# A lag of six and eight pieces behind the first token half, the turn of h ahead of the last step, and a shorter expert selection

## The reference, cut to what matters

```python
merged = sigmoid(ga) * (ya @ w_branch_a) + sigmoid(gb) * (yb @ w_branch_b)
mix_out = merged @ w_out
ple = sigmoid(x @ w_ple_gate) * (p @ w_ple)
x = layer_norm(ALPHA * x + mix_out + ple, ln_g, ln_b)      # end of block 1
h = rms_norm(x, g_mix_norm) * (1 + scale_m) + shift_m      # block 2 begins
q_lat, kv_lat, k_rope, fq, fk, fv, f_logit, gate_a, gate_b = split(h @ w_in)
```

```python
choice = sigmoid(h @ w_router) + b_router
group_keep = top 4 of (sum of the two best choices in each group)
expert_idx = top_k(where(group_keep, choice, -1e30), 6)
```

## Time and profile before

| | |
|---|---|
| median of 3 runs | 1021.34 us (1021.08 to 1021.52) |
| the profiled execution | 1018.69 us, its span 1017.0 us |
| PE busy | 995.1 us (98%) |
| DVE, ACT, POOL busy | 586.9, 441.1, 380.0 us |
| mean granted TensorE clock | 0.998 of full |
| HBM read | 319.25 MB, 316 GB/s over the span |

### The profile page before, as it was taken

How to read it: one execution, slowest core, us unless ns; L and a number is a source line. 1 busy time by engine, 2 the same in 40 slices (tenths; PEclk the granted TensorE clock), 3 DMA queues, 4 the chain that set the end, 5 groups by cost and what they waited for, 6 DMA issues and landing times.

```text
span 1017.0 us, 14499 instructions
## 1 busy us (share of the span) xinstructions
PE 995.1 (98%) x5866; PEld 707.9 (70%) x5866; DVE 586.9 (58%) x1032; ACT 441.1 (43%) x731; POOL 380.0 (37%) x363
## 2 busy tenths in 40 slices
PE   9999999999999899999999999999999999999997
PEld 7878888888887787888787665655555564655553
DVE  4899768877966796866666333433333332333353
ACT  5645777656434664667344232222322232222213
POOL 2299999995993089698001100000000000000000
PEclk9999999999999999999999999999999999999999
DMA  9767666567675386565589899999999999999994
GB/s 330 310 223 252 231 208 231 209 215 285 232 239 203 140 301 211 203 202 170 196 329 407 351 426 428 423 427 427 426 427 426 426 424 428 425 429 423 427 425 180
DMA packets 36260, 322.31 MB, mean 317 GB/s; under 512 B 4160, under 2 KB 4192, under 8 KB 13664
## 3 DMA queue, kind: packets, MB, share of 16 engines
q1 hardware_dynamic: 28064, 291.94, 71.7%
q0 software_dynamic: 7840, 28.90, 8.7%
q10 hardware_dynamic: 288, 0.52, 0.1%
HBM read 319.25 MB, written 2.10 MB: 316 GB/s over the span
## 4 chain that ended last, share of the span: by engine, by line
PE 86%; DVE 7%; ACT 3%; DMA 2%; issue 1%; SPq 1%; ACTq 0%; DVEq 0%
PE ps L931 77%; PE ps L1312 6%; PE ps L935 4%; DVE rlo L1879 3%; DVE rt L1879 1%; DMA ring<-in_w_in 1%; ACT hl L1435 1%; DMA ring<-in_w_out 1%; DVE bs L1879 1%; ACT ex L1435 0%; DVE L L1879 0%; ACT L L1435 0%; SPq L803 0%; SPq L804 0%; ACT bs L1435 0%
## 5 line engine op out<-in xcount | busy, mean ns | idle before, releaser
L931 PE MATMUL ps<-hl,L 128*128 128x512 f32 (+1 forms) x1216 | 329.9, 393 | 5.1 <-DVE L L1879 4.1
L931 PEld LDWEIGHTS ps<-hl,L 128*128 128x128 f32 x1216 | 225.1, 188 | 54.5 <-issue 7.0
L1879 DVE TENSOR_TENSOR rlo<-ring,hl 128x1024 fp32r<-128x1024 f32 (+1 forms) x154 | 219.6, 1445 | 71.5 <-ACT hl L1435 70.8
L931 PE MATMUL ps<-slots_all,xe 128*64 128x256 f32 x2048 | 228.1, 381 | 0.0
L1435 ACT ACTIVATE hl<-ring 128x1024 fp32r<-128x1024 f32 (+1 forms) x154 | 160.3, 1055 | 115.3 <-PE ps L931 105.9
L931 PEld LDWEIGHTS ps<-slots_all,xe 128*64 128x64 f32 x2048 | 144.2, 137 | 74.6 <-issue 5.0
L931 PE MATMUL ps<-rlo,L 128*128 128x512 f32 (+1 forms) x608 | 187.5, 389 | 1.1 <-DVE rlo L1879 0.9
L859 POOL TENSOR_SCALAR mring<-mring,st 128x512 f32<-128x512 f32 x84 | 167.4, 1993 | 1.6
L931 PEld LDWEIGHTS ps<-rlo,L 128*128 128x128 f32 x608 | 113.8, 188 | 26.5 <-DVE rlo L1879 3.1
L921 POOL CAST two<-ident 64x64 fp32r<-64x64 f32 x104 | 20.5, 239 | 293.2 <-PE ps L931 275.6
L861 POOL TENSOR_TENSOR macc<-macc,mring 128x512 f32<-128x512 f32 x84 | 126.8, 1509 | 7.0
(11 more groups left out here) (248 smaller groups left out, 886.1 us busy)
## 6 DMA issues: line engine op xcount, KB each, us to landing
slots_all<-in_w_exp_gate SPq DMA_DIRECT2D x32, 2048.0 KB, 25.3
slots_all<-in_w_exp_up SPq DMA_DIRECT2D x32, 2048.0 KB, 26.7
slots_all<-in_w_exp_down SPq DMA_DIRECT2D x31, 2048.0 KB, 28.0
ring<-in_w_in SPq DMA_DIRECT2D x48, 1024.0 KB, 4.9
mring<-in_w_mod POOLq DMA_DIRECT2D x48, 512.0 KB, 4.0
ring<-in_w_out SPq DMA_DIRECT2D x8, 1024.0 KB, 7.1
ring<-in_w_ple_gate SPq DMA_DIRECT2D x4, 1024.0 KB, 5.6
ring<-in_w_branch_a SPq DMA_DIRECT2D x4, 1024.0 KB, 5.5
```

The source lines that it names most:

```text
L931: return e.matmul(o, l, r, start=start, stop=stop)
L1879: return e.tensor_tensor(o, a, b, op)
```

## The change

It does these things:

1. Two more `hl` buffers (`hl_more`) for all pieces up to `g0`, so eight instead of six; `ready_with` is worked out with them, so up to `g0` each conversion stands up to two pieces earlier in the streams of ACT and DVE.
2. `wo0 wo1` at a lag of 6 (14 steps); `c0` and `fq` become one run with a lag of 8 (16 steps).
3. PE: `merged_turn(1)` after step 4 of `wo`; `h_turn(0)` after step 12, ahead of the last half-piece; `mod_sum(9)` after the run; the six unread matmuls go; `h_turn(1)` after step 6 of the joined run.
4. ACT and DVE: their parts of the layer norm stand at other steps; the evacuations of `c0` and `fq` move inside the joined run, and the norm of the latents comes behind all its 16 steps.
5. `h3_turn(0)` after step 10 of `wp`, ahead of the last half-piece; `h3_shift` in two parts of two columns.
6. Selection: `pen` and one product fall away, ranks count from 1 instead of 0 so that a subtraction goes, selectors before the copy of the ranks, and `gather(0, 0..3)` ahead of `turn_ranks`.

```diff
+        hl_more = place("hl_more", [128, 2, 1024], F32R, at=pos[0])
-        BEHIND = (("bb0 bb1", 4), ("wo0 wo1", 4), ("c0", 4), ("om0 om1", 3), ("wp0 wp1", 4))
+        BEHIND = (("bb0 bb1", 4), ("wo0 wo1", 6), ("c0 fq", 8), ("om0 om1", 3), ("wp0 wp1", 4))
...
+        more_until = blocks["g0"][0]
+        hi_buf = [g % (NH + 2) if g < more_until else (g - npieces + 4) % NH for g in range(npieces)]
+        hi_before = [max((q for q in range(g) if hi_buf[q] == hi_buf[g]), default=None) for g in range(npieces)]
...
-            while at_piece < npieces and (at_piece < NH or used[at_piece - NH] < t) and all(
+            while at_piece < npieces and (hi_before[at_piece] is None or used[hi_before[at_piece]] < t) and all(
                     freed_by(q) <= t for q in range(pieces[at_piece][0] - NS + 1)):
...
-            project("wo0", L1, l_ready("mT"), {1: lambda: merged_turn(1)})
+            project("wo0", L1, l_ready("mT"), {4: lambda: merged_turn(1), 12: lambda: h_turn(0)})
             mod_sum(9)
-            h_turn(0)
-            w.wait_ge(*evacuated(two_before["c0"], 0))
-            for n in range(6):
-                mm(PS[bank_of["c0"]][:, 0:128], ident[:, :], ident[:, :], True, True)
-            project("c0", L0, h_ready, {2: lambda: h_turn(1)})
-            project("fq", L0, h_ready)
+            project("c0", L0, h_ready, {6: lambda: h_turn(1)})
             project("fk", L0, h_ready)
...
-            h3_turn(0)
+            project("wp0", L0, l_ready("mT2"), {1: lambda: merged_turn2(1), 10: lambda: h3_turn(0)})
...
+            gather(0, range(4))
             turn_ranks()
-            gather(0, range(4))
...
-            project("wo0", at={2: first_rows, 7: lambda: ln_square(0), 8: first_squares, 9: roots})
+            project("wo0", at={5: first_rows, 7: lambda: ln_square(0), 8: first_squares, 9: lambda: square_root(0)})
             h_round(0, 0)
+            ln_square(1)
             h_round(0, 4)
...
+            project("c0", at={3: second_rows, 6: second_h, 12: lambda: keep("c0", lambda m: PR[:, m, :], ACT.Copy)})
+            fox("fq", FQ)
...
+            project("wo0", at={3: lambda: wo(0, 0), 5: lambda: completed("mT", tokens=(1,)), 7: first_rows, 9: first_root,
+                               13: lambda: h_shift(0)})
+            wo(1, 1)
+            less_mean(1)
+            h_low(0, 0)
+            variance(1)
+            h_shift(4)
+            scale(1)
+            scaled(1, 0)
+            h_low(0, 4)
+            scaled(1, 1)
+            mod_sum(9)
...
+            project("c0", at={3: second_root, 5: lambda: pr_evac(0, PS[bank_of["c0"]][:, :]), 6: second_h,
+                              9: lambda: fox_evac("fq", FQ)(0, PS[bank_of["fq"]][:, :])})
...
-            mine(tt(kp, gsb[:, :, 0:8], gs[:, :, 0:8], ALU.not_equal))
-            mine(tsc(pen, kp, 1.0, 1e30, ALU.subtract, ALU.mult))
-                x = tt(w8[m], c8[m], spread(kp[:, m, :], 8), ALU.mult)
-                x = tt(w8[m], w8[m], spread(pen[:, m, :], 8), ALU.add)
+            mine(tt(left_out, gsb[:, :, 0:8], gs[:, :, 0:8], ALU.is_equal))
+                x = stt(w8[m], spread(left_out[:, m, :], 8), -1e30, c8[m], ALU.mult, ALU.add)
...
-            tsc(RK, RK, 1.0, None, ALU.subtract, None).then_inc(rk_set, 1)
```

More of the change, by code:

```diff
@@ L325, in two_blocks @@
         two_before = {name: order[n - 2] if n > 1 else None for n, name in enumerate(order)}
+        more_until = blocks["g0"][0]
+        hi_buf = [g % (NH + 2) if g < more_until else (g - npieces + 4) % NH for g in range(npieces)]
+        hi_before = [max((q for q in range(g) if hi_buf[q] == hi_buf[g]), default=None) for g in range(npieces)]
+        last_more = max(g for g in range(more_until) if hi_buf[g] >= NH)
         def hi_of(g):
-            return hl[:, (g - npieces + 4) % NH, 0:2 * pieces[g][2]].rearrange("p (k n) -> p k n", k=2)
+            b = hi_buf[g]
+            v = hl[:, b, :] if b < NH else hl_more[:, b - NH, :]
+            return v[:, 0:2 * pieces[g][2]].rearrange("p (k n) -> p k n", k=2)
         def ring_pair(i):
@@ L789, in load_early @@
                 if q == "shared":
+                    w.wait_ge(pe_w, both(last_more))
                     e.dma_start(w_shared, D["w_route_2"]).then_inc(shared_in, 16)
@@ L1541, in project @@
                         w.wait_ge(*((halves_in[i], 16) if g in (0, 2) else (slot_sem[i % NS], slot_at[i])))
-                        if g >= NH:
-                            w.wait_ge(pe_w, both(g - NH))
+                        if hi_before[g] is not None:
+                            w.wait_ge(pe_w, both(hi_before[g]))
                         act(hi_of(g), view, ACT.Copy).then_inc(hi, 1)
@@ L1659, in first_squares, with second_rows, second_h, fox @@
                 square(0, 1)
[L1661 to L1665 removed]
+            project("wo0", at={5: first_rows, 7: lambda: ln_square(0), 8: first_squares, 9: lambda: square_root(0)})
             h_round(0, 0)
[L1667 removed]
+            ln_square(1)
             h_round(0, 4)
[L1669 to L1673, removed]
+            def second_rows():
+                square(1, 0)
+                square(1, 1)
+                square_root(1)
+            def second_h():
+                h_round(1, 0)
+                h_round(1, 4)
+            project("c0", at={3: second_rows, 6: second_h, 12: lambda: keep("c0", lambda m: PR[:, m, :], ACT.Copy)})
+            def fox(name, buf):
+                if name != "fq":
+                    project(name)
+                done(name, 1)
+                act(heads(buf, 1, 66)[:, :, 0:64], PS[bank_of[name] + 1][:, :].rearrange("p (h d) -> p h d", d=64),
+                    ACT.Copy).then_inc(ev_a.sem, 1)
+            fox("fq", FQ)
             for base_ in (64, 136):
@@ L1676, in _ @@
                 act(st[:, base_ + 4:base_ + 6], st[:, base_ + 4:base_ + 6], ACT.Sqrt).then_inc(lat_a, 1)
-            def fox(name, buf):
-                project(name)
-                done(name, 1)
-                act(heads(buf, 1, 66)[:, :, 0:64], PS[bank_of[name] + 1][:, :].rearrange("p (h d) -> p h d", d=64),
-                    ACT.Copy).then_inc(ev_a.sem, 1)
             w.wait_ge(fz_v, 1)
@@ L2374, in first_rows, with first_root, second_root @@
                 scaled(0, 1)
-            def second_rows():
+            def first_root():
                 w.wait_ge(sq_a, 2)
                 mean_square(0, rt_v)
-                wo(1, 1)
+                wo(0, 1)
                 diagonal(0)
[L2381 to L2392, removed]
+            project("wo0", at={3: lambda: wo(0, 0), 5: lambda: completed("mT", tokens=(1,)), 7: first_rows, 9: first_root,
[10 more added lines that the diff above has]
+            mod_sum(9)
+            def second_root():
                 w.wait_ge(sq_a, 4)
@@ L2395, in third_rows, with second_h @@
                 diagonal(1)
[L2397 to L2400, removed]
+            def second_h():
+                h_low(1, 0)
+                h_low(1, 4)
             def pr_evac(m, b):
```

64 lines of the change are left out of this document (26 added, 38 removed).

## The result

The changed kernel takes 1036.74 us in the median of 4 runs (1034.21 to 1037.93); the kernel before took 1021.21 beside it (4 runs, 1019.57 to 1021.52). The ratio is 1.0148, 95% interval 1.0126 to 1.0171. The forecast was 1030.0 with a range of 1022.0 to 1035.5: the direction is right, the time lies above the range. The profiled execution took 1034.21 us, its span 1032.5 against 1017.0, and its mean granted clock is 0.988 against 0.998.

A forecast was written before the change was run, and what follows sets the result against it. PE was taken as the bound, busy 995.1 of 1017.0 us. Terms 4.3 + 0.6 - 0.7 + 4.3 + 1.0 - 0.75 = +8.75 on 1018.69 gave 1027.4, plus 2.65 to the median 1030.1, stated as 1030.0; range 1022 to 1035.5.

The forecast's parts named there:

- part 4: Latents: `lT` waits 4.1 us for the late norm, `fv` starts 4.3 later, `latents_up` another 1.0 later.
- F+15.4: Time counted from F, the start of `fk`: from about there DVE has four conversions, an evacuation and LT before `latents_up`.
- a rival with a chance of 0.12: Clock falls to half in PE's stops before `c0` and `lT`: up to +5 us on the sum, up to 1035; chance 0.12.
- two stops of 4 us: PE waits 4.0 us before `c0` and 4.1 before `lT`, both forecast in the sum.
- `c0` to `fk`: Joined run of `c0` and `fq`: 24.36 us before, 2.4 of waits become 1.7, so -0.7.
- My price per fall: Loss from one clock fall, 2.5 us, from 30 small matmuls at the start taking 6.25 us; two falls up to +5.
- start to `wo0`: Conversion of `wo1` waits for its load ahead of rounding `mT`: `wo0` starts at 318.3 instead of 313.98, +4.3.
- my own lower case of +1.5: The delay of `wo0` if loads land after 4.9 us instead of 7.7: +1.5 instead of +4.3.
- `wo0` to `c0`: 26.6 us of work, 1.7 of waiting before `h_turn(0)` and a 4.0 hole before `c0`: 32.3 against 31.65, +0.6.
- `h3_turn(0)`: In `wp`, one half-piece earlier: `wp(1,1)` comes 0.94 later, but the chain to `h3_turn(1)` has slack: 0, bound -0.9 to +0.9.
- selection's term: Fewer small operations before the ranks (0.33 us) and no 0.40 wait before `turn_ranks`: -0.75, lost again if expert loads come no earlier.
- the lags themselves: Without both +4.3 terms +0.9 is left, total +0.15: lags alone bring nothing, as the DVE queue keeps the rows back.

The follow-up runs named there:

- sixth: Changed kernel, but a piece is converted no sooner than 5 half-pieces after its slot was freed, unless PE needs it at the next step: 1026.62 us, ratio 1.0057.
- second: Changed kernel with matmuls that nothing reads, 15 in front of `c0` and 19 in front of `lT`: 1034.34 us, ratio 1.0146.
- eighth: Changed kernel with the edits of the sixth and the seventh together: 1027.56 us (7 runs), ratio 1.0052.
- fifth: Changed kernel with the two added buffers placed 32 bytes further on: 1035.95 us, ratio 1.0139.
- seventh: Changed kernel with the norm of the latents at step 12 of the joined run instead of behind all 16 steps: 1036.12 us, ratio 1.0154.
- ninth: Changed kernel with all pieces ahead of `wo0` converted at the steps of the kernel before: 1035.24 us, ratio 1.0144.
- tenth: Changed kernel without the earlier `h3_turn(0)`, plus edits of fifth, sixth, seventh and ninth, and `h_low(0, 0)` ahead of `less_mean(1)`: 1022.90 us, ratio 1.0020.
- fourth run: Kernel before with only `h3_turn(0)` one half-piece earlier and `h3_shift` in two parts: 1020.19 us, ratio 1.0008.

## Why the prediction was wrong

**Right: the direction and the mechanism.** Conversions stand ahead of the layer norm and wait for their loads. Moving them back alone (sixth) returns about 10 of 15.5 us, and the buffers alone (first) cost 8.8.

Between the forecast and the trace lie 6.75 us. By the rows of the table they are -0.46, -0.32, +1.97, +3.13, +1.43, +1.04 and -0.04. Two steps failed: the chain of DVE behind the latents, and the clock, which I had put at nothing in the sum.

**Wrong, the largest part: the chain from `fk` to `latents_up`,** +9.86 where part 4 had +5.3. Its start, the load, was right. Then I counted one load where the third piece waits for the next one: 1.1 us. Behind the norm I had the four conversions start at F+15.4, and they start at F+18.4; the other 1.9 of that are mostly the wait for ACT and its two table loads, which stand nowhere in the forecast. And I took 1.22 us for a conversion on DVE, with the 1.45 of the earlier trace rows explained as waits of operands: the four took 6.88, 2.0 more. Of these 5.0 us 4.6 show, as my sum left some slack. The explanation by waits was a misreading, and the trace of before could have told me. Of its 154 conversions on DVE, the 41 with no computing instruction of POOL's beside them took at most 1.23 us; the 85 that ran beside one of its TENSOR_TENSOR took up to 2.35. The half clock in this stretch cost nothing that lasted, since `latents_up` starts on DVE's last row.

**Wrong: the clock left out of the sum.** I made it a rival with a chance of 0.12, to be added if it comes, and wrote against it that today's gap is filled and no row shows a gap of this length. But the forecast itself had two stops of 4 us with nothing in them. The clock fell at three places. In `c0` it cost 1.95 us: `c0` to `fk` took 23.68 in the traces of the second, sixth and eighth run, where the clock holds, and 25.53 to 25.64 in the four traces with the hole of 4.2 us and a fall (changed kernel, fifth, seventh, ninth). Before `lT` it cost nothing, as said. In the end of the block it cost 1.7. Together that is 3.6 us, about half of the miss. The Trainium skill ("TensorE: Matmul & The Clock Gate", section "Why this matters for your kernels") warns of just these gaps, and the trace agrees that the clock falls in them; its rule should have gone into the sum with the price of a fall, not beside it. My price per fall, 2.5 us from the earlier trace rows, was above the 1.95 and 1.7 measured. It also rested on taking the first matmuls to run at the lower level, which the earlier trace rows don't show; the windows of the trace of before read 1.00 from 1 to 8 us.

**Right number, partly by luck: start to `wo0`,** +4.3 forecast, +3.84 measured. 1.77 us had been lost before `merged_turn(0)`, of which I allowed 0 to 1, and only 2.07 came by the stop that I had at 4.3. My argument for the first was that ACT's waits have a margin before PE needs the pieces. It overlooked that evacuations of PE's banks stand in the same queues. The second is the load's time to landing, 5.0 us where I had 7.7 and said that the issue wouldn't move; it is near my own lower case of +1.5. The ninth shows that the early loss isn't additive, as it is mostly waited for in front of `wo0` otherwise. `wo0` to `c0` (+0.6 forecast, +0.28 measured) has the same small luck: one wait was 0.9 shorter than forecast, the other 0.3 longer.

**Right at full clock: `c0` to `fk`.** -0.7 forecast makes 23.66 us, and the traces without a fall have 23.68. What made it +1.27 is the fall, and some 0.1 us of the added buffers at 0.03 to 0.04 us a half-piece, which nothing in the trace of before could show.

**Overlooked: `h3_turn(0)`.** I took it as 0 with a bound of 0.9. The chain is indeed no longer, but it gathers two short waits into one of 2.23 us, and that cost the clock in five traces of eight, 1.7 us each time. The selection's term (-0.75) came as -0.71 in the trace. The row `latents_up` to `gate_up` shows only 1.04 of difference because 0.7 us were gained before `h3_turn(0)`, which I hadn't forecast.

**Of the lags themselves** I said that they bring nothing because DVE keeps the rows back. With the conversions moved, `wo0` to `fk` takes 51.7 us in the eighth run against 56.0 before, and in the tenth `c0` starts 4.2 us sooner. They do bring something; what kept the rows back was for the most part conversions ahead of them in DVE's queue.

Left open: how often the stops at 204 and 271 us come, and how far they make the spread of the runs; why the wait before `lT` was 8.13 us in one trace; and why 32 bytes matter.

## What to carry to other kernels

When more buffers let work start earlier in an in-order queue, ask what the load needs after its issue: work taken up before its data is there holds all that is written behind it, and that may be the critical chain or the emptying of a bank. Where a forecast has a stop of several us on the matrix engine, the clock's fall belongs into the sum, but only where nothing else ends later than the slow stretch: here it cost 1.95, 1.7 and 0 us. Two short waits can be better than one long, as the end of the block shows. A mean duration above the shortest one is a question to ask of the rows, not a wait to be taken off. And when a block is joined or moved, look for every wait that counts from its end: one line of POOL's was worth 4.8 us.

## What the runs showed of the hardware

- An operand 32 bytes off: matmuls of 512 columns out of buffers on a multiple of 64 bytes (from the start of the kernel's memory) take 1.39 to 1.40 us per six, those 32 bytes further on 1.36.
- A wait of 2.23 us in front of small matmuls was followed by half clock in five traces and by full clock in three. Behind a wait of 1.15 us (fourth run, 422.55) the clock fell too, and behind one of 1.13 at the same place in the trace of before it didn't.
- DVE's operations with two inputs took up to 3.5 times as long beside a busy POOL (1.49 instead of 0.42 us, eighth run), and a conversion up to 2.35 us instead of 1.23 (trace of before).
- A stretch at half clock can be free: from 389.1 to 399.4 us in the changed kernel's trace it delayed nothing that lasted, since DVE's chain ended later than PE's.
- A filling of small matmuls kept the clock at 1.00 up to a wait of 0.72 us, but not over two more waits of 1.58 and 0.83.
